# Modulation rows loaded on SyncE's queue between the weights, and another order of VectorE's work ahead of three projections

## What is computed

```python
# first block: attention and convolution mixer, modulated by c, then a gated FFN with a convolution
mod = silu(c) @ ada_w + ada_b                      # 1024 x 6144, split into sh1, sc1, g1, sh2, sc2, g2
h = rms_norm(x, norm1_g) * (1 + sc1) + sh1
q, k, v, gb, gc, xs = split(h @ w_in + b_in)       # then rope, sliding-window attention, 3-tap convolution
x = x + g1 * (concat(rms(y_attn), rms(y_conv)) @ w_o)
x = x + g2 * ffn_conv(rms_norm(x, norm2_g) * (1 + sc2) + sh2)
x = rms_norm(x, final_norm_g)
# second block: RWKV-7 time mixing + SwiGLU, then a spatial gating unit + SwiGLU
for mixer in (rwkv7, sgu):
    x = x + rmsnorm(mixer(rmsnorm(x)))
    x = x + rmsnorm(swiglu(rmsnorm(x)))            # d_ff = 2816
```

## Time and profile before

| | us |
|---|---|
| median of 3 runs | 2181.41 |
| lowest and highest | 2180.72, 2184.52 |
| the profiled execution | 2181.41 |
| its span | 2179.4 |

### The profile page before, as it was taken

One profiled execution on the slowest core, in us unless ns is written; L12 is line 12 of the kernel. 1 busy time (PEld: TensorE's weight loads), 2 busy tenths in 40 slices (PEclk: granted clock), 3 DMA queues, 4 the chain that ended last, 5 costly groups with the idle time before them and its releaser, 6 DMA issues.

```text
span 2179.4 us, 35358 instructions
## 1 busy us (share of the span) xinstructions
PE 2014.1 (92%) x14379; PEld 1574.9 (72%) x14379; DVE 1081.7 (50%) x1573; ACT 785.0 (36%) x1243; POOL 239.1 (11%) x269
## 2 busy tenths in 40 slices
PE   7998989999997998899978999999899789999997
PEld 5776768888882666677756788888667558888885
DVE  6677765445227543587743544432353544444323
ACT  4334233333221334577633333322243443323221
POOL 1100000000023000222211011110000011111100
PEclk8989989999998999799989999999999989999998
DMA  8544223333321222000002233343133023333320
GB/s 293 174 123 127 80 68 89 94 96 109 103 78 41 78 78 60 7 9 9 7 23 78 67 96 97 97 116 93 52 84 99 21 58 92 97 97 100 114 79 39
DMA packets 311050, 180.98 MB, mean 83 GB/s; under 512 B 16381, under 2 KB 303763, under 8 KB 310932
## 3 DMA queue, kind: packets, MB, share of 16 engines
q1 hardware_dynamic: 305506, 162.29, 25.5%
q0 software_dynamic: 4608, 16.78, 2.5%
q10 hardware_dynamic: 818, 0.21, 0.0%
HBM read 177.16 MB, written 2.10 MB: 82 GB/s over the span
## 4 chain that ended last, share of the span: by engine, by line
PE 61%; DVE 5%; issue 4%; ACT 2%; POOL 1%; DVEq 0%; ACTq 0%; POOLq 0%
PE bank L247 16%; PE bank L248 16%; PE bank L249 16%; PE bank L1947 4%; PE bank L441 1%; DVE rstd L351 1%; PE bank L1744 1%; PE bank L2428 1%; PE bank L2422 1%; PE bank L2529 1%; POOL gsq L1449 0%; PE bank L2639 0%; PE bank L2640 0%; PE bank L2614 0%; PE bank L2488 0%
## 5 line engine op out<-in xcount | busy, mean ns | idle before, releaser
L232 DVE TENSOR_TENSOR wlo<-raw,whi 128x1024 fp32r<-128x1024 f32 (+1 forms) x262 | 340.3, 1299 | 759.4 <-ACT whi L226 759.2
L226 ACT ACTIVATE whi<-raw 128x1024 fp32r<-128x1024 f32 (+1 forms) x262 | 293.2, 1119 | 771.2 <-PE bank L249 764.1
L247 PE MATMUL bank<-fh_hi,whi 128*128 128x512 f32 x1056 | 420.8, 398 | 24.3 <-DVE fh_lo L415 16.8
L248 PE MATMUL bank<-fh_lo,whi 128*128 128x512 f32 x1056 | 414.9, 393 | 0.0
L249 PE MATMUL bank<-fh_hi,wlo 128*128 128x512 f32 x1056 | 414.9, 393 | 0.0
L247 PEld LDWEIGHTS bank<-fh_hi,whi 128*128 128x128 f32 x1056 | 199.1, 189 | 82.4 <-DVE fh_lo L415 27.7
L248 PEld LDWEIGHTS bank<-fh_lo,whi 128*128 128x128 f32 x1056 | 199.4, 189 | 44.6 <-issue 2.0
L249 PEld LDWEIGHTS bank<-fh_hi,wlo 128*128 128x128 f32 x1056 | 199.3, 189 | 44.2
L248 PE MATMUL bank<-f_lo,whi 128*128 128x512 f32 x528 | 205.4, 389 | 0.0
L247 PE MATMUL bank<-f_hi,whi 128*128 128x512 f32 x528 | 205.4, 389 | 0.0
L249 PE MATMUL bank<-f_hi,wlo 128*128 128x512 f32 x528 | 205.4, 389 | 0.0
(11 more groups left out here) (407 smaller groups left out, 3058.4 us busy)
## 6 DMA issues: line engine op xcount, KB each, us to landing
raw<-in_w_up_dram SPq DMA_DIRECT2D x44, 512.0 KB, 3.8
raw<-in_ffn_w_gate_dram SPq DMA_DIRECT2D x44, 512.0 KB, 3.8
raw<-in_ffn_w_up_dram SPq DMA_DIRECT2D x44, 512.0 KB, 3.8
raw<-in_ffn_w_down_dram SPq DMA_DIRECT2D x32, 704.0 KB, 4.6
late<-in_ada_w_dram POOLq DMA_DIRECT2D x32, 512.0 KB, 4.2
raw<-in_rwkv_w_rkv_dram SPq DMA_DIRECT2D x24, 512.0 KB, 4.0
raw<-in_w_down_dram SPq DMA_DIRECT2D x16, 704.0 KB, 4.6
early<-in_ada_w_dram SPq DMA_DIRECT2D x16, 512.0 KB, 14.9
```

The costliest lines, as they stand in the source:

```text
L226: act.activation(whi[:, at.slot, 0:kts * P], raw_unit(at, kts), ACT.Copy).then_inc(hi_ready, 1)
L232: dve.tensor_tensor(wlo[:, at.slot, 0:kts * P], raw_unit(at, kts), whi[:, at.slot, 0:kts * P].bitcast(F32), ALU.subtract).then_inc(lo_read ...
L247: pe.matmul(dst, hi, rhs_hi(k), start=first and k == 0, stop=False)
L248: pe.matmul(dst, hi, rhs_lo(k), start=False, stop=False)
```

## The change

There are two edits.

The first: `pool_late` is gone. One list, `plan`, now holds the weight units of the first mixer and the late tiles in the order in which SP issues them, and each late DMA carries the same waits that it had on GpSimd. After each even unit below 12 two late tiles follow, after each odd one and after units 12 to 17 one, and after each unit of `w_o` one. The slots and their numbers are the same, and so is the work of all other engines.

The second: in `Lead.dve` the addition of tile k - 1 now follows the scaling of tile k, and the low half that follows is that of tile k - 2.

```diff
--- before.py
+++ after.py
@@ -450,13 +450,27 @@
     w_in, w_o, ada_w = (A[n].rearrange("a k n -> (a k) n") for n in ("w_in", "w_o", "ada_w"))
     N_IN, N_O = 18, KD
     EARLY = 2 * KD
+    order, m = [], EARLY
+    for u in range(N_IN):
+        order.append(("in", u))
+        for _ in range(2 - u % 2 if u < 12 else 1):
+            order.append(("late", m))
+            m += 1
+    for u in range(N_O):
+        order.append(("o", u))
+        if m < 6 * KD:
+            order.append(("late", m))
+            m += 1
     at_in, at_o, seq = {}, {}, []
-    u_next = 0
-    for kind, n in [("in", u) for u in range(N_IN)] + [("o", u) for u in range(N_O)]:
-        at = At(len(seq), u_next)
-        seq.append((kind, n, at))
-        {"in": at_in, "o": at_o}[kind][n] = at
-        u_next += 1
+    u_next, plan = 0, []
+    for kind, n in order:
+        at = None
+        if kind != "late":
+            at = At(len(seq), u_next)
+            seq.append((kind, n, at))
+            {"in": at_in, "o": at_o}[kind][n] = at
+            u_next += 1
+        plan.append((kind, n, at))
     first = [at for _, _, at in seq]
     for n in range(2):
         first.append(At(len(seq) + n, u_next + n))
@@ -503,7 +517,14 @@
             sp.dma_start(x_tok[:, t, :], x_in[t]).then_inc(x_landed, 16)
         for m in range(EARLY):
             sp.dma_start(early[:, m, :], ada_rows(m)).then_inc(early_landed[m], 16)
-        for kind, n, at in seq:
+        for kind, n, at in plan:
+            if kind == "late":
+                if n == EARLY:
+                    sp.wait_ge(x_turned, KD)
+                if n >= EARLY + RAW:
+                    sp.wait_ge(*ada_used(n - RAW))
+                sp.dma_start(late[:, n % RAW, :], ada_rows(n)).then_inc(late_landed[n % RAW], 16)
+                continue
             freed = None
             if at.c >= RAW:
                 freed = (lo_ready, seq[at.c - RAW][2].count)
@@ -516,14 +537,6 @@
             else:
                 parts = unit_parts(at, w_in, (0, KD), in_columns(n))
             load(sp, at, parts, freed)
-
-
-    def pool_late(pool):
-        pool.wait_ge(x_turned, KD)
-        for n in range(EARLY, 6 * KD):
-            if n >= EARLY + RAW:
-                pool.wait_ge(*ada_used(n - RAW))
-            pool.dma_start(late[:, n % RAW, :], ada_rows(n)).then_inc(late_landed[n % RAW], 16)
 
 
     setup = ExitStack()
@@ -1254,8 +1267,11 @@
             for k in range(KD):
                 self.res.scale(dve, k)
                 if k >= 1:
-                    self.half.dve_lo(dve, k - 1)
-                self.res.add(dve, k)
+                    self.res.add(dve, k - 1)
+                if k >= 2:
+                    self.half.dve_lo(dve, k - 2)
+            self.res.add(dve, KD - 1)
+            self.half.dve_lo(dve, KD - 2)
             self.half.dve_lo(dve, KD - 1)
 
         def act(self, act):
@@ -3040,7 +3056,6 @@
     @block.gpsimd
     def _(pool):
         pool_setup(pool)
-        pool_late(pool)
         ffn0.pool_gained_sum(pool)
         pool_masks(pool)
         pool_blocks(pool)
```

## The result

| | before | after |
|---|---|---|
| median, us | 2181.76 (4 runs) | 2203.08 (4 runs) |
| lowest and highest | 2180.72, 2184.52 | 2199.04, 2204.81 |
| profiled execution, span | 2181.41, 2179.4 | 2205.03, 2203.1 |

The ratio is 1.0093, 95% interval 1.0075 to 1.0111. The ratio makes it 20.3 us slower, the medians are 21.3 us apart; 17.1 were forecast (16.9 by the sum). The profiled execution is 2 us above the median of its kernel, so the stages read from it add up to 23.6 us, more than the medians show.

What follows compares the result with a forecast made beforehand. TensorE, busy for 92% of the span, was taken as the bound. Moving the loads (14.8 us) and the reorder (2.1) sum to 16.9 us on 2181.41: 2198.3, given as 2198.5, own range 2193 to 2204, 8 in 10 within 2189 to 2208.

Steps and rivals of the forecast that it cites:

- The ring: Projection prologue: split, rotation, accumulate, late load, weight load and next unit's split wait in turn, 11.0 us against 6.34.
- the load pair: Prologue, SP's queue: a late load and the weight load behind it land in 3.8 + 1.7 = 5.5 us.
- the first two rivals: Prologue load pair takes 3.8 us, total 2191.7 (chance 0.15); or 7.6 us, total 2206.7 (chance 0.12).
- A sign: Prologue timeline: TensorE should show gaps of some 5 us before units 4 and 5.
- The third rival: Moving the late loads to SP is free and only the reorder counts: 2183.0 us, chance 0.03.
- Nothing given back, nothing added behind: Attention steps and output units after the prologue: the 14.3 us lost are neither recovered nor added to.
- part A: Late loads moved from GpSimd's queue to SP's, felt in the prologue: 14.3 + 0.5 = 14.8 us slower.
- The first link: Prologue, accumulate 16 to unit 3's split: 5.5 us for loads plus 1.16, split at 66.8, +5.3 us.
- the last link: Prologue, accumulate 22 to unit 7's split: 5.5 us for loads plus 1.16, split at 101.2, +14.3 us.
- The small gain ahead: Prologue start: VectorE's second split no longer holds back the modulation add, 0.5 us gained or nothing.
- The clock behind K's rotation: Start of the attention steps: slow TensorE products at the 1.2 GHz level lose 0.5 us, from 0 to 3.5.
- Part B: New Lead.dve order at three leads: first low half 0.94 us later, 0.7 us lost each, 2.1 in all; lower bound 0.

Runs made afterwards that it cites:

- Weights first: Changed kernel's loads with the old Lead.dve order; of each pair one accumulate releases, the weight load goes out before the late load; 2191.99 us, one run.
- waits only: Kernel before, late loads still on GpSimd; SP only waits ahead of each weight load for the same accumulate as in the changed kernel; ratio 1.0068.
- spaced: Changed kernel with late loads on SP placed so no weight load waits longer than for its own slot; old Lead.dve order; ratio 0.9995.
- one unit later: Changed kernel's load order with each late load one weight unit further back; old Lead.dve order; ratio 0.9997.
- Unit 7 ahead: Changed kernel's loads with old Lead.dve order, but unit 7 issued ahead of late load 26 instead of behind it; 2206.14 us, one run.
- loads only: Changed kernel with the old order in Lead.dve, so only the late loads are moved to SP; ratio 1.0074.
- before again: Kernel before, unaltered, run once more for a second profile; 2182.49 us.
- after again: Changed kernel, unaltered, run once more for a second profile; 2210.18 us.
- reorder only: Kernel before with only the new order of Lead.dve, late loads left on GpSimd; ratio 0.9998.
- spaced and reordered: Changed kernel, new Lead.dve order kept, late loads on SP placed so no weight load waits longer than for its own slot; ratio 1.0019.
- switch: Kernel before with the old Lead.dve order up to tile 3 and the new one from tile 4 on; 2177.99 us, one run.
- low half one later still: Kernel before with each low half in Lead.dve behind the scale three tiles on; 2187.22 us, one run.

## Why the prediction was right, and where its sizes were off

**The ring: right in its terms, the load pair's with some luck.** 1.14 + 1.93 + 1.31 + 5.57 + 1.16 = 11.11 us at unit 4, forecast 1.14 + 1.93 + 1.3 + 5.5 + 1.16 = 11.0. That the load pair takes 3.8 + 1.7, and not 3.8 or 7.6, was the choice on which the first two rivals hung. The 5.5 was right, its source was not: the two loads of the earlier trace rows were issued 1.6 us apart and took 5.5 and 5.6 us each, so that their landings are 1.7 us apart shows when they were issued and not what a load adds right behind another. In the changed kernel the late load lands 3.6 us after its issue and the weights 2.0 us after that. Weights first takes the late transfer out of the link and has 9.7; waits only has it on another queue and has 9.7 and 9.8.

**A sign that came by half.** I expected TensorE's gaps to be some 5 us before units 4 and 5. They were 4.50 and 2.00, with the rest of unit 5's in products at the 1.2 GHz level, and 5.37 came before unit 7.

**The waits and not the transfers: shown.** Waits only loses 15.4 us at K's rotation with every transfer on the engine where it was; spaced and one unit later move all transfers and lose nothing. The third rival's sentence, with the rule of the Trainium skill in "DMA: Bandwidth & Descriptors", section "Issuing engines are not separate DMA queues", is half right. The trace agrees so far that the issuing engine matters little to the transfer (the late loads' median to landing is 3.9 us from SP in after and in spaced, 4.2 from GpSimd), and the move was free in the two orders in which no wait ahead of a weight load ends too late. The section says nothing of such waits, and they made the difference.

**Nothing given back, nothing added behind: right but for the clock.** TensorE was 15.1 us behind at 300 us and 15.5 at 1000, then 22.8 at 1190, through the clock.

**The mis-sized terms of part A.** The first link: unit 3 is loaded in two DMAs, which took 1.67 us to issue, and its weights were there 6.2 us after the late load (60.14 to 66.30), not 5.5: 0.7 us. That the two DMAs are the reason is read from the rows, and no run tests it. The last: 7.5 us, not 5.5, since I let the pair of unit 7 start on an empty queue. In the order SP has a late load 1.4 us ahead of the pair. Together with 0.1 in the ring this makes the split of unit 7 at 103.97, not at 101.2, and K's rotation 17.1 us late, not 14.3. Unit 7 ahead shows the loads ahead as a part of the last link's excess: with one load ahead instead of two the weights landed in 5.0 us, against 7.1 in after and 6.2 in loads only.

**The small gain ahead: not shown.** I took 0.5 us off, since the modulation add would no longer wait for VectorE's second split. That split is out of the way (40.1 us instead of 42.69), but TensorE's sums start 0.45 us later, at 40.08, and the add starts at 43.69 instead of 43.83. Accumulate 16 did end at 60.11, as forecast, and TensorE was 0.5 us ahead at 60; but before again is 0.4 ahead there with no edit, and after again 1.7 behind. So the term is within what differs from one execution to the next.

**The clock behind K's rotation.** The clock there, which I had at 0.5 us of loss, gave 2.0 back in this execution; loads only and waits only got nothing back (17.2 and 15.4 at 300 us), after again 1.8, and before again gained 4.2 with no ring at all. So I don't put it down to the edit.

**Part B: right in kind, smaller in the leads.** The first low half came 0.93 us later (forecast 0.94) and the idle time of VectorE was not recoverable: it grew. Of the 0.7 us per lead, 0.53, 0.52 and 0.62 were paid in the reorder alone, 0.37, 0.42 and 0.56 between spaced and spaced and reordered. In the changed kernel the leads are 24.74, 24.84 and 25.37. Executions with the old order and a slow stretch of the same length, 10.2 us, have 24.75, 24.76 and 24.72 (before again) and 24.67 and 24.76 (the first two of loads only). So there it cost nothing, 0.1 and 0.65 us. The first two would fit the lower bound that I named, a shift inside time that TensorE loses to the half clock; but after again, with stretches of 10.2 us there too, has 24.99 and 25.02, 0.25 us more than before again. A single lead is no measure of a few tenths: with the old order's start the first two leads lie between 24.63 and 25.10 us, and the third is once 25.32 (one unit later). The three leads together are 74.4 us in the mean of the nine profiles with the old order's start and 75.8 in the four with the new order, 1.4 us more. By the leads part B is worth 0.8 to 1.7 us and not 2.1. The times say 0 (reorder only), some 4 us (the changed kernel against loads only, 1.0093 and 1.0074) and some 5 us (1.0019 against 0.9995), the latter two with intervals that overlap. What they hold beyond the leads isn't shown; in the profiles the 3.4 us stretches of the gate stage, at half clock 1.7 us each, would be a part of it.

**The forecast was 4.6 us low.** 2.8 is unit 3's and unit 7's links; the leads are 0.4 to 1.3 the other way. The rest is put down to TensorE's clock: in the profile, which is itself 2 us above the median, 7.3 us between 1000 and 1190, 1.5 at the gate, 2.0 back in the steps. No term of the sum was for these stretches. Waits only, with nearly the same ring, has no such stretch at 1043 and is at 15.4 to 17.4 us throughout.

**Open.** What brings the stretches. That at 1043 to 1076 us was 10 to 14 us long in after and in five experiments (loads only, unit 7 ahead, reorder only, spaced, spaced and reordered), the last three of which have no loss in the prologue at all; it was absent in before, waits only and switch, and 3.4 us long in before again, after again, one unit later, weights first and the low half one later still. So it varies by execution, and I can't say whether the edits make it more likely. Those of the gate stage came once in after, after again, loads only and unit 7 ahead, twice in reorder only and in spaced and reordered, and never in before, before again, spaced, one unit later, waits only, weights first, switch and the low half one later still; one profile of each doesn't settle whether the reorder brings them. No version was shown to be faster than before: spaced and one unit later are level with before, the single 2177.99 of switch was not repeated.

## What to carry to other kernels

Before a transfer is moved to another engine's list, write down for each transfer behind it which earlier event it now waits for, and how many units of lead are left; part A was lost by one place in a list, and one place back made it free. Where two loads are let go by the same event, issue the one on the path first: it was worth 1.3 us a turn here. In these leads a reorder cost at its start, and VectorE's idle time beside the ring was no reserve for it.

## What the runs showed of the hardware

- Loads of 512 KB from SP's queue one behind the other, in the prologue of after and loads only: alone 3.6 to 3.9 us to landing, the second 0.4 us behind the first 5.0 to 5.2 (5.4 to 5.6 from the first's issue), the third, with the others 1.8 and 0.4 us ahead, 7.1 in after and 6.2 in loads only.
- Two queues at once: in waits only unit 7's load from SP, with one of GpSimd's 1.1 us ahead and one 0.3 behind, took 7.9 us. In weights first, with all three on SP's queue, the others 1.4 us ahead and 0.4 behind, it took 5.4. It is one run of each.
- Executions of one and the same kernel differ in how long TensorE's clock is at the 1.2 GHz level between 1043 and 1190 us of before's time: 20.5 and 27.3 us in the two profiles of before, 34.1 and 41.0 in the two of after. Against before's first profile they took 4.0 us from before's second, 7.3 from the first of after and 9.7 from its second (1000 to 1190 us), as much as many an edit is worth; a distance between two profiles is best read where it begins.
- At the start of a lead the stretch at the 1.2 GHz level was either some 13.7 us or some 10.2 us long, in either order of the work.
